# Adding weighted expert rows into a residual kept in memory, instead of storing a row per pair and summing at the end

## The reference

```
h  = rmsnorm(x1, g_ffn)
lg = h @ router_group_w + b;   p_top, g = top-1 of softmax(lg)          # 4 groups
le = (h @ router_expert_w + b)[group g];  v2, e = top-2 of le           # 8 experts a group
w2 = softmax(v2) * p_top                                                # two weights a token
for each token and each of its 2 experts:  act = silu(h @ w_gate) * (h @ w_up)     # 128 wide
                                           out = (act * weight) @ w_down
x  = x1 + sum of the token's two expert rows
y  = rmsnorm(x, g_final)
```

## Time and profile before

| | |
|---|---|
| three runs | 624.71, 626.22, 628.14 us (median 626.22) |
| profiled execution | 624.81 us, span of the instructions 623.1 us |
| granted TensorE clock, mean | 0.989 |
| busy: PE, PEld, DVE, ACT, POOL | 95%, 81%, 76%, 46%, 17% |
| DMA | 115.99 MB; HBM read 99.90 MB, written 20.68 MB |
| GpSimd's indirect DMAs | 35 gathers (L1141), 35 scatters (L1156) |
| expert loop, first gather to last scatter | 379.6 to 583.3 us |
| last stage | 585.7 to 623.1 us |

### The profile page before, as it was taken

One profiled execution on the slowest core, in us unless ns is written; L12 is line 12 of the kernel. 1 busy time (PEld: TensorE's weight loads), 2 busy tenths in 40 slices (PEclk: granted clock), 3 DMA queues, 4 the chain that ended last, 5 costly groups with the idle time before them and its releaser, 6 DMA issues.

```text
span 623.1 us, 10651 instructions
## 1 busy us (share of the span) xinstructions
PE 590.8 (95%) x3539; PEld 503.2 (81%) x3539; DVE 474.5 (76%) x742; ACT 283.9 (46%) x439; POOL 106.9 (17%) x151
## 2 busy tenths in 40 slices
PE   8999999999999999899999976999999999999765
PEld 6899999997998898788888756888888888887222
DVE  4938997999999687456566587898787878787177
ACT  6642112230313337222321146777777777775434
POOL 4300001000000000000000004133344444443100
PEclk9999999999999999999999987999999999999998
DMA  8760210221113203654112238999999999983398
GB/s 309 147 141 15 67 36 0 68 57 35 35 43 112 77 17 106 187 224 169 67 69 79 73 125 314 320 352 361 345 322 375 372 390 361 374 319 113 89 420 361
DMA packets 53512, 115.99 MB, mean 186 GB/s; under 512 B 10627, under 2 KB 28936, under 8 KB 52361
## 3 DMA queue, kind: packets, MB, share of 16 engines
q1 hardware_dynamic: 46069, 96.90, 44.9%
q0 software_dynamic: 6784, 17.84, 8.3%
q10 hardware_dynamic: 596, 0.50, 0.3%
HBM read 99.90 MB, written 20.68 MB: 194 GB/s over the span
## 4 chain that ended last, share of the span: by engine, by line
PE 53%; DVE 15%; DMA 5%; issue 3%; ACT 2%; POOLq 2%; POOL 1%; SPq 1%; DVEq 0%; ACTq 0%
PE ps L2095 13%; PE ps L1917 8%; PE ps L2244 7%; PE ps L2221 4%; PE ps L2220 4%; PE ps L2222 4%; PE ps L2198 4%; DMA at_opair_p<-scratch_out 3%; DVE at_mixP L1288 2%; PE ps L2159 2%; POOLq L1123 1%; DVE at_hT L1247 1%; DVE at_lnsq L1474 1%; PE ps L2318 1%; PE ps L1845 1%
## 5 line engine op out<-in xcount | busy, mean ns | idle before, releaser
L1917 PE MATMUL ps<-at_hT,at_ring 128*128 128x384 f32 x936 | 165.5, 333 | 0.0
L1917 PEld LDWEIGHTS ps<-at_hT,at_ring 128*128 128x128 f32 x936 | 155.9, 188 | 5.1 <-issue 5.0
L2095 PE MATMUL ps<-at_hT,at_mring 128*128 128x512 f32 (+1 forms) x432 | 102.7, 393 | 1.9 <-DVE at_mring L1442 1.2
L2095 PEld LDWEIGHTS ps<-at_hT,at_mring 128*128 128x128 f32 (+1 forms) x432 | 77.3, 182 | 21.1 <-DVE at_mring L1442 1.7
L2220 PE MATMUL ps<-at_whi,at_hTm 128*128 128x256 f32 x280 | 81.0, 289 | 0.0
L1288 DVE SCALAR_TENSOR_TENSOR at_mixP<-at_uc,sb_par,at_mixP 128x1024 f32<-128x1024 f32 x60 | 77.3, 1289 | 2.1
L2222 PE MATMUL ps<-at_whi,at_hTm_lo 128*128 128x256 f32 x280 | 78.2, 279 | 0.0
L1683 DVE TENSOR_TENSOR at_wlater_lo<-at_wlater,at_whi 128x1024 fp32r<-128x1024 f32 x40 | 49.0, 1224 | 9.2 <-ACT at_whi L926 6.8
L1667 DVE TENSOR_TENSOR at_hTm_lo<-ps,at_hTm 128x1024 fp32r<-128x1024 f32 x34 | 41.6, 1224 | 18.4 <-ACT at_hTm L910 17.8
L2220 PEld LDWEIGHTS ps<-at_whi,at_hTm 128*128 128x128 f32 x280 | 52.8, 188 | 0.0
L2222 PEld LDWEIGHTS ps<-at_whi,at_hTm_lo 128*128 128x128 f32 x280 | 52.5, 188 | 0.0
(11 more groups left out here) (274 smaller groups left out, 903.5 us busy)
## 6 DMA issues: line engine op xcount, KB each, us to landing
at_wlater<-in_expert_w_gate SPq DMA_DIRECT2D x20, 512.0 KB
at_wlater<-in_expert_w_up SPq DMA_DIRECT2D x20, 512.0 KB
at_wlater<-in_expert_w_down SPq DMA_DIRECT2D x20, 512.0 KB
at_raw<-in_w_in SPq DMA_DIRECT2D x16, 512.0 KB, 3.9
at_opair_p<-scratch_out SPq DMA_DIRECT2D x8, 1024.0 KB, 14.5
at_wfirst<-in_expert_w_gate SPq DMA_DIRECT2D x15, 512.0 KB
at_wfirst<-in_expert_w_up SPq DMA_DIRECT2D x15, 512.0 KB
at_wfirst<-in_expert_w_down SPq DMA_DIRECT2D x15, 512.0 KB
```

Of the source, the lines that this page charges most:

```text
L1917: mm = pe.matmul(ps[:, bank + r, 0:t1 - t0], w[:, wpart, k * P:(k + 1) * P], hT[:, hpart, k, t0:t1], start=(m, wpart, hpart) == (0, 0, 0), ...
L2095: mm = pe.matmul(ps[0:n, b + r, :], mring[:, 1 - i % 2, mpart, k * P:k * P + n], wo[:, wpart, k, r * 512:(r + 1) * 512], start=(c, mpart, ...
```

## The change

Each pair now has its own row in `scratch_h`, 1,025 wide: the 1,024 values, stored twice a token, and the pair's gate in the last column. The gather takes this row by pair (`tab`), the gate lands with it, and `expert_act` multiplies by it. `scratch_out` has one row a token, holds `x1` before the first scatter, and each scatter adds to it. As a token may stand in two blocks, each scatter waits until the one before has landed. The gates are computed in the tile loop and before the first expert, on POOL and ACT, in two parts (tiles 0 to 5, and 6 to 8). The last stage loads a row a token. The core of the diff:

```
+GATE_PARTS = [(0, 6), (6, TILES)]                     # FINAL is now 0..8 in order
-        xg = at("xg", [P, XG, D], o_xg)
+        xg = at("xg", [P, XG, D + 1], o_xg)
-        hs = nc.dram_tensor("scratch_h", [NT, D], F32, kind="Internal").ap()
-        orow = nc.dram_tensor("scratch_out", [2 * NT, D], F32, kind="Internal").ap()
+        hs = nc.dram_tensor("scratch_h", [2 * NT, D + 1], F32, kind="Internal").ap()
+        orow = nc.dram_tensor("scratch_out", [NT, D], F32, kind="Internal").ap()
 SP, store_h2 (doubled) and store_x1 (new, after each store_h2; the last after block 5's weights):
+                dst = hs[2 * i * P:2 * (i * P + n), 0:D].rearrange("(t k) d -> t k d", k=2)
+                src = wk[0:n, 2 if i == LAST else i % 2, 0:D].unsqueeze(1).broadcast_to([n, 2, D])
+            def store_x1(i):
+                sp.wait_ge(s["x1_ready"], i + 1)
+                sp.dma_start(orow[i * P:i * P + rows(i), :], x1[0:rows(i), i, :])\
+                    .then_inc(s["x1_stored"], 16)
 SP, last stage:
-                src = orow[2 * i * P:2 * (i * P + n), :].rearrange("(t k) d -> t (k d)", k=2)
-                sp.dma_start(opair(i)[0:n, :], src).then_inc(pair_in[i], 16)
+                sp.dma_start(x1[0:n, i, :], orow[i * P:i * P + n, :]).then_inc(sum_in[i], 16)
 ACT (gate_exp(0) behind square(7, 1), gate_exp(1) between the zero fills of xg, store_gates(0, 0, 6) in
 the round of tile 8, store_gates(1, LAST, TILES) and (1, 6, LAST) behind the zero fills):
+            def gate_exp(part):
+                t0, t1 = GATE_PARTS[part]
+                act.wait_ge(s["gex_in"], part + 1)
+                do(A(gex[:, t0:t1, :], gex[:, t0:t1, :], ACT.Exp), s["gex_out"])
+            def store_gates(part, t0, t1):
+                act.wait_ge(s["gates_ready"], part + 1)
+                for k in range(1 if t0 == LAST else 2):
+                    if t0 == LAST:
+                        dst = hs[2 * LAST * P:2 * NT, D:D + 1].rearrange("(p k) o -> p (k o)", k=2)
+                        src = gates[0:NS, LAST, :]
+                    else:
+                        dst = hs[2 * t0 * P:2 * t1 * P, D:D + 1]\
+                            .rearrange("(i p k) o -> k p (i o)", p=P, k=2)[k]
+                        src = gates[:, t0:t1, k]
+                    act.dma_start(dst, src, allow_slow_non_contiguous=True).then_inc(s["gates_in"], 16)
+            do(A(xg[:, :, D], ones[:, 0:XG], ACT.Copy, scale=0.0))
 POOL (gate_terms(0), gate_values(0) before rms of tiles 7 and 8, part 1 behind the last rms):
+            def gate_values(part):
+                t0, t1 = GATE_PARTS[part]
+                do(g.memset(gates[:, t0:t1, 1], -1.0))
+                pool.wait_ge(s["gex_out"], part + 1)
+                second, top = gex[:, t0:t1, NG], gates[:, t0:t1, 0]
+                do(g.tensor_tensor(gex[:, t0:t1, 0:2], gex[:, t0:t1, 0:2], gex[:, t0:t1, 2:4], ALU.add))
+                do(g.tensor_tensor(gsum[:, t0:t1], gex[:, t0:t1, 0], gex[:, t0:t1, 1], ALU.add))
+                do(g.tensor_scalar(top, second, 1.0, 1.0, ALU.mult, ALU.add))
+                do(g.tensor_tensor(top, top, gsum[:, t0:t1], ALU.mult))
+                do(g.tensor_tensor(top, top, gates[:, t0:t1, 1], ALU.pow))
+                do(g.tensor_tensor(gates[:, t0:t1, 1], top, second, ALU.mult), s["gates_ready"])
 gather (index is now tab, bounds_check last_pair):
-                        pool.wait_ge(s["xt_done"], free)
+                        pool.wait_ge(s["act_ready"], free)
 scatter:
+                    if b == 0:
+                        pool.wait_ge(s["x1_stored"], 16 * TILES)
+                        pool.wait_ge(s["tok_ready"], 1)
+                    else:
+                        pool.wait_ge(scat[(b - 1) % 2], 16 * ((b - 1) // 2) + 16)
+                    g.indirect_dma_start(orow, bass.IndirectOffsetOnAxis(ap=token[0:n, :], axis=0),
+                                         outb[0:n, b % 2, :], None, bounds_check=last_token,
+                                         oob_is_err=False, compute_op=ALU.add)\
+                        .then_inc(scat[b % 2], 16)
 before gather 0:
+            pool.wait_ge(s["gates_in"], 16 * 5)
 DVE, expert_act:
-                v.tensor_tensor(actv[:, j % 2, :], sg[:, j % 2, :], ps[:, 2 + j % 2, FF:2 * FF],
-                                ALU.mult).then_inc(s["act_ready"], 1)
+                v.scalar_tensor_tensor(actv[:, j % 2, :], ps[:, 2 + j % 2, FF:2 * FF],
+                                       xg[:, j % XG, D:D + 1], sg[:, j % 2, :],
+                                       ALU.mult, ALU.mult).then_inc(s["act_ready"], 1)
 DVE and PE: the gates behind the loop, add_experts, own_rows, the diagonal products and dg are gone;
 for each tile ACT squares x1 when it has landed, DVE norms it.
```

More of the change, by code:

```diff
@@ L317, in build_layer @@
         h2_stored = [sem(f"h2_stored{i}") for i in range(2)]
-        pair_in = [sem(f"pair_in{i}") for i in range(TILES)]
+        sum_in = [sem(f"sum_in{i}") for i in range(TILES)]
         def wait_piece(eng, p):
@@ L1023, in final_root @@
                    s["y_root"])
[L1026 to L1031, removed]
             do(A(acts[:], epsc[:], ACT.Sqrt))
             for i in FINAL:
[L1034 to L1041, removed]
+                act.wait_ge(sum_in[i], 16)
+                square(i, 2)
                 final_root(i)
@@ L1148, in gather, with scatter @@
                 else:
-                    by_size(pairs, move)
-            def scatter(b, index):
+                    by_size(index, move)
+            def scatter(b, token, index):
                 def move(n):
@@ L1182, in _ @@
                     c = n * CAPB
-                    gather(n, gidxs[:, c:c + 1], tab[:, c:c + 1], b + 1 if b >= 0 else None)
+                    gather(n, tab[:, c:c + 1], b + 1 if b >= 0 else None)
                 else:
@@ L1191, in _ @@
                     c = (b - 1) * CAPB
-                    scatter(b - 1, tab[:, c:c + 1])
+                    scatter(b - 1, gidxs[:, c:c + 1], tab[:, c:c + 1])
             def all_scattered(n):
@@ L1779, in _ @@
                                 expert_out(i + NE // LAP, j, bank=0)
-            dve.wait_ge(s["gex_out"], 1)
-            do(v.tensor_reduce(gsum[:], gex[:, :, 0:NG], AX_X, ALU.add))
-            do(ts(gates[:, :, 0], gex[:, :, NG], 1.0, None, ALU.add))
-            do(tt(gates[:, :, 0], gates[:, :, 0], gsum[:], ALU.mult))
-            do(v.reciprocal(gates[:, :, 0], gates[:, :, 0]))
-            do(tt(gates[:, :, 1], gates[:, :, 0], gex[:, :, NG], ALU.mult), s["gates_ready"])
-            dve.wait_ge(s["moe_done"], 1)
-            dve.wait_ge(s["gain_fin_in"], 16)
-            def add_experts(i):
-                n = rows(i)
-                dve.wait_ge(pair_in[i], 16)
-                for k in range(2):
-                    do(stt(x1[0:n, i, :], opair(i)[0:n, k * D:(k + 1) * D],
-                           gates[0:n, i, k:k + 1], x1[0:n, i, :], ALU.mult, ALU.add),
-                       s["y_sum"] if k == 1 else None)
+            dve.wait_ge(s["gain_fin_in"], 16)
             def final_norm(i):
@@ L1805, in final_norm @@
                 do(v.reciprocal(rs[0:n, 2, i:i + 1], rs[0:n, 2, i:i + 1]))
-                x, g, y = x1[0:n, i, :], gain[0:n, :], x1[0:n, i, :]
-                if i in PE_TILES:
-                    x = sum_banks(PE_TILES.index(i))
-                    g, y = (z.rearrange("p (b c) -> p b c", b=2) for z in (g, y))
-                do(stt(y, x, rs[0:n, 2, i:i + 1], g, ALU.mult, ALU.mult), s["y_done"])
-            add_experts(8)
-            final_norm(8)
-            add_experts(1)
-            final_norm(0)
-            final_norm(1)
-            final_norm(2)
-            add_experts(3)
-            add_experts(7)
-            final_norm(3)
-            final_norm(4)
-            final_norm(7)
-            final_norm(5)
-            final_norm(6)
+                do(stt(x1[0:n, i, :], x1[0:n, i, :], rs[0:n, 2, i:i + 1], gain[0:n, :],
+                       ALU.mult, ALU.mult), s["y_done"])
+            for i in FINAL:
+                final_norm(i)
         @block.tensor
```

97 lines of the change are left out of this document (41 added, 56 removed).

## The result

The changed kernel takes 684.41 us (median of 5 runs, 681.46 to 685.64) against 625.86 us before (5 runs beside it, 624.08 to 628.14): ratio 1.094, 95% interval 1.0915 to 1.0966. Slower, as forecast, but by 58.5 us and not by 5, and outside the range of 616 to 660. The profiled execution took 681.46 us, its span is 679.6 us, 56.5 more than before.

What follows compares the result with a forecast made beforehand. The prediction took TensorE as the bound until about 583 us and DMA bytes from 585.7 us. Its terms, +2.7 + 12 + 1.5 - 11 = +5.2 us, on 624.8 gave 630.0 us (631.4 against the median), range 616 to 660.

Steps and rivals of the forecast that it cites:

- the chain of scatters: Expert loop: each scatter waits for the one before to land, binding in 14 late steps; +12 us, bounds 0 and +65.
- L + 0.8: Expert loop: period of chained scatters, start-to-landing time L plus GpSimd's 0.8 us; 5.05 us early, 6.6 late.
- the landing of a plain scatter: Expert loop: interpolated by rows between 2.44 us and 6.8 for 128 rows; 3.85 us early, 2.44 + 2.6 late.
- The addition's second read: Expert loop: an accumulating scatter also reads the destination row; 0.4 us early, 0.75 late in each landing.
- My other rows, 6.7 and 6.9 us: Expert loop before the change: landings of plain scatters 28 and 29, with DMA half idle; 6.8 taken for 128 rows.
- rival B: Expert loop: the waits between scatters are hidden, an accumulate landing in under 4.7 us; -6.8 us, 619.4, chance 0.32.
- Bytes of the loop: Expert loop: 8.9 MB of extra reads put off the last weights by 8 to 10 us, covered by prefetch; 0.
- The other case of the prediction: Expert loop: an accumulate three times a plain row, a further 9 MB or 22 us that prefetch would not cover.
- The start: Before the first expert: gates must be in memory, so gather 0 starts at 382.3 us; +2.7, bounds +1.4 and +6.
- the last stage: After the experts: one row per token read instead of one per pair, 26.7 us; gain 10.7 to 13.3, taken as 11.
- the end of the experts: Last two scatters: 33 and 34 follow each other by a landing, and the last lands 0.5 us later; +1.5 us.
- Rival C: Expert loop: accumulates last about 6.8 us at most blocks, period 7.6, weights late too; +40 to +60, 675 us, chance 0.13.

Runs made afterwards that it cites:

- number 4: Changed kernel with experts taken in turn from the four groups, only the overflow blocks' scatters still waiting for the one before: 640.01 us, ratio 1.0222.
- number 2: Changed kernel with scatters writing rows instead of adding, still each waiting for the one before, the sum left out: 657.28 us, ratio 1.0484.
- number 1: Kernel before, its plain scatters into a row per pair, each waiting until the one before has landed: 657.52 us, ratio 1.0505.
- numbers 3: Changed kernel with scatters adding into a row per pair without waiting for the one before, the sum of two rows left out: 639.76 us, ratio 1.021.
- numbers 8: Changed kernel with expert groups in turn and, from block 8 on, only an eighth of each down matrix loaded: 624.47 us, ratio 0.9983.
- 9: Kernel before with only an eighth of each down matrix loaded from block 8 on, as control: 625.26 us, ratio 1.0004.
- number 10: Changed kernel with expert groups in turn and scatters writing rows instead of adding, the sum left out: 622.68 us, ratio 0.9946.
- number 5: Changed kernel with SP loading the weights of blocks 4 and 5 only once the gates are in memory: 682.48 us, ratio 1.0891.

## Why the prediction was wrong

**The step that failed** is the chain of scatters, "I take +12, bounds 0 and +65". The mechanism was named and is the cause: taking the wait away, and nothing from the additions, brings 44 us back (number 4). The size was off: 58.3 us in the loop, near the upper bound. I had put L + 0.8 at 5.05 us early and 6.6 us late; measured are 106.7 / 15 = 7.1 and 128.4 / 17 = 7.6 us. Of its terms, the landing of a plain scatter was the wrong one: forecast 3.85 us early and 2.44 + 2.6 = 5.04 late, measured in number 2 as 99.1 / 15 - 0.8 = 5.8 and 116.4 / 17 - 0.8 = 6.0, in number 1 as 5.8 and 5.7. So it passed the 4.7 us that a step hides in the early small blocks too, on average, and the chain bound there as well and not only in 14 late steps.

- I took the landing to depend on the rows of a block. It depends also on what else the DMA engines carry. Number 1 shows it with plain stores: 3.37 to 3.64 us for a full block near the end, where the share is 0.29; in the 17 steps, with the share at 0.96 from 470 to 540 us, 5.7 us on average. The row that I interpolated from, 2.44 us, was taken beside idle engines and stood for blocks of the loop.
- The addition's second read, counted as bytes, was not what failed in the loop: forecast 0.4 and 0.75 us, measured 0.5 and 0.7 (number 2). Beside idle engines it is another size: 2.5, 2.9 and 1.4 us for the three full blocks of number 2. Why it adds less where the load is higher is open.
- My other rows, 6.7 and 6.9 us, were read as the price of one full block. GpSimd's timeline before the change around the second:

```profile
562.24 1.23 POOL L1156 DMA_INDIRECT scratch_out<-at_outb,at_tab  x1 [0.30 <-issue]
564.10 0.99 POOL L1156 DMA_INDIRECT scratch_out<-at_outb,at_tab  x1 [0.63 <-issue]
```

Another scatter started 1.9 us behind it, before it had landed; the first, of 555.37, had the last weights beside it (share 0.50 until 562.08). Alone and with those gone, a full plain block lands in 3.4 to 3.6 us (number 1). How much of the difference is the overlap and how much the load was not separated. The upper end of my range came near the truth partly by luck: too long for a plain store by itself, about right for an addition.

The page "DMA: Bandwidth & Descriptors" of the Trainium skill (Anatomy of one DMA, SWDGE path) has 2.0 us plus bytes at 436 GB/s; the estimate by it is 3.0 us for some 110 plain rows of 4 KB. The trace of number 1 comes near it with idle engines (3.37 to 3.64) and not in the loop (5.7), and additions are outside it. It spoke for rival B; that rival was wrong.

**Bytes of the loop**, taken as 0 because the prefetch covers them, is the second mis-sized term. It hid behind the chain; without it, it is 15.8 us (numbers 3 and 4), and numbers 8, 9 and 10 show that it is the additions' engine time. The price of the reads was right: q0 takes 11.7% of 637.0 = 74.5 us of all engines in number 4 and 8.3% of 621.0 = 51.5 in number 10, so 23 us, against 8.9 MB at 416 GB/s = 21.4. What failed is the cover. "To 470 us the engines have room" took the rate, 346 GB/s, for the load, while the share in the same row was 1.01 already. From 400 to 470 us, at a share of 0.99 to 1.01, number 10 moves 350 GB/s and number 4 317: what the additions take, the weights lose from the start. The other case of the prediction, an accumulate of three times a plain row, is not what happened. With half of the 51.5 us put down to the scatters (an estimate), an addition takes 1.9 times as long as a plain row.

**The start**: forecast +2.7, bounds 1.4 to 6, measured +6.35 at gather 0 and +8.1 at the first scatter. Gates were ready at 375.5 (forecast 376.3), their last store was issued at 377.4 (377.5), but landed at 384.9, not 381.5: the upper case, queueing behind weights, held. It is gather 0 at 385.93 instead of 379.58. The other 1.8 us come behind it: TensorE now stands for 8.17 us before its first transposes instead of 2.05, and its granted clock is 0.57 from 384 to 396 us, near the lower of its two levels (1.2 GHz), against 0.98 from 380 to 392 before, near the upper (2.4 GHz). The 16 transposes took 3.65 us, where two groups of eight had taken 1.13 and 1.15 (the last two rows below, from the kernel before).

```profile
390.83 3.65 PE L2212 MATMUL ps<-sb_ident,at_xg 128*128 128x128 f32 x16 [8.17 <-DMA at_xg<-scratch_h,at_tab]
```

```profile
384.36 1.13 PE L2198 MATMUL ps<-sb_ident,at_xg 128*128 128x128 f32 x8 [2.05 <-DMA at_xg<-scratch_h,at_gidxs]
385.90 1.15 PE L2198 MATMUL ps<-sb_ident,at_xg 128*128 128x128 f32 x8 [0.41 <-DMA at_xg<-scratch_h,at_gidxs]
```

That the longer wait is what lowered the clock is not shown. In number 1, where nothing differs before the first scatter, the same 16 transposes took 3.22 us behind only 1.83 us of idle time, at a clock of 0.65 from 386 to 390 us, and the first scatter started 1.45 us later than before. So a part of the 1.8 us may come and go without the change.

That stores of single elements are slow by their number is not what this case shows: the Trainium skill's page "DMA: Bandwidth & Descriptors" (Rules for kernel authors) gives one descriptor for each element, which I had put on the side of the upper bound, but alone they landed 1.9 to 2.0 us after their issue (number 5).

**Right were**: the last stage, 26.5 us against 26.7 forecast, with nothing for the work removed from TensorE and VectorE; the end of the experts, 0.8 + 0.9 = 1.7 against 1.5; the gather's later wait and VectorE's new product (0.34 us instead of 0.28) at nothing, since the loop of number 10 takes 186.0 us against 185.1.

**The chances** were wrong too. Rival C, the long landing at most blocks, got 0.13 because it needed "6.8 at each block", and I gave 0.32 to the one that needed the row taken beside idle engines. In a stretch where the DMA share is 1.01 to 1.02 the rows of a loaded moment were the nearer ones. C's 675 us, with its period of 7.6, was within 10 us.

**Left open**: numbers 1 and 2 have the same chain of plain stores, but their 17 steps take 109.8 and 116.4 us; wider gather rows, the later gather and the start differ, and no run parts them. No version with the whole computation beats the kernel before. Number 10, without the sum, is 0.5% faster; it says what the rest of the change is worth: 10.9 to 11.3 us of last stage, less 8 of start.

## What to carry to other kernels

A wait that orders DMAs one behind another turns landing time into a period: price it with a landing seen under the load of that very stage, for every block, and compare it with the step it must hide under. An addition in memory saves a later read but is paid in DMA engine time that the byte counts do not show; here its hidden read cost about what plain bytes cost (23 us against 21.4). And look for room in the share of busy time, not in the distance to the highest rate: at a share of 1.01 with 346 GB/s there was none. If updates must not meet, order the work so that neighbours can't (here, expert groups in turn, 44 us) before ordering the DMAs.

## What the runs showed of the hardware

- An adding indirect DMA of some 110 rows of 4 KB lands after 5.4 to 6.3 us beside mostly idle engines, a plain one after 3.3 to 4.1 (changed kernel and number 2); with few rows, the last ones land after 3.34 and 2.45 us. Issuing it keeps GpSimd busy for 1.44 instead of 0.94 us. In a chain beside the weights the addition costs only 0.5 to 0.7 us a step.
- Plain scatters land after 3.4 to 3.6 us at a DMA share of 0.29 and after 5.7 us on average at 0.96 (number 1).
- 70 gathers and scatters of the same 17.8 MB took 8.3 to 9.3% of the engines' span as plain ones and 11.6 to 13.2% with additions, over all kernels here; the queue's bytes do not show the second read. With nothing else changed (numbers 4 and 10) it is 74.5 against 51.5 us of all engines.
- Three stores of single 4-byte elements (640 in all) land 1.9 to 2.0 us after their issue alone (number 5) and up to 8.1 us after it behind expert weights (changed kernel).
